# Output-projection units inside an SSM scan's end, and a re-ordered index stage with the first attention pair in it

## The reference

```
first block, layer 0 (mamba2):  z, xbc, dt = split(rmsnorm(x) @ w_in);  xbc = silu(conv4(xbc))
    y  = chunked scan over 4 chunks of 128 tokens, 8 groups of 4 heads, + d_skip * xs
    out = rmsnorm(y * silu(z)) * gate_norm @ w_out          # 2048 -> 1024, "ssm_out"
second block, layer 1 (sparse attention, 528 tokens = 16 meta + 512):
    q, k, v, qi, ki, wi = split(rms_norm(h) @ w_in)         # 16 heads of 64; 8 index heads of 64
    score = sum_h relu(qi_h . ki / 8) * wi_h                # causal; the 16 meta tokens always win
    top   = the 128 best keys of each query;  softmax attention over these alone
```

## Time and profile before

| | us |
|---|---|
| median of three timed runs | 2241.99 (2241.15 to 2243.61) |
| the profiled execution | 2250.37 |
| its span, first to last instruction | 2248.6 |
| TensorE busy | 2140.4 |
| VectorE busy | 1460.2 |
| ScalarE busy | 1022.7 |

### The profile page before, as it was taken

The page is one execution under the profiler, slowest core; times in us unless marked ns, Lnnn a source line. Parts: engine busy times, 40 slices in busy tenths (PEclk is TensorE's granted clock), DMA queues, the critical chain, the costliest instruction groups (busy, mean ns, idle before and its releaser), DMA issues. The chain is left out here.

```text
span 2248.6 us, 40146 instructions
## 1 busy us (share of the span) xinstructions
PE 2140.4 (95%) x14761; PEld 1871.6 (83%) x14761; DVE 1460.2 (65%) x3068; ACT 1022.7 (45%) x1893; POOL 79.3 (4%) x101
## 2 busy tenths in 40 slices
PE   6999999999999799999999999989999999999998
PEld 4777777777767688889999999977877789999886
DVE  6687877537775777776676653369467776666632
ACT  4555554435654456665443332324455554443322
POOL 1000000000000011100000000122100000000000
PEclk9999999999999999999999999988999999999999
DMA  5533331253211222222333243401111213333331
GB/s 129 137 99 104 97 93 52 75 112 66 48 38 57 66 76 66 69 82 58 90 88 93 84 113 88 99 19 38 53 38 37 75 48 95 93 93 90 106 90 50
DMA packets 354767, 174.71 MB, mean 78 GB/s; under 512 B 61055, under 2 KB 350696, under 8 KB 354664
## 3 DMA queue, kind: packets, MB, share of 16 engines
q1 hardware_dynamic: 351976, 168.19, 27.3%
q0 software_dynamic: 2688, 5.20, 1.0%
HBM read 166.58 MB, written 2.16 MB: 75 GB/s over the span
## 5 line engine op out<-in xcount | busy, mean ns | idle before, releaser
L307 PE MATMUL ps<-h_parts,parts 128*128 128x264 f32 (+3 forms) x8576 | 1307.5, 311 | 18.7 <-DVE h_parts L682 6.3
L307 PEld LDWEIGHTS ps<-h_parts,parts 128*128 128x128 f32 x8576 | 1171.3, 190 | 112.0 <-issue 19.4
L266 ACT ACTIVATE parts<-ring 128x1024 fp32r<-128x1024 f32 (+1 forms) x284 | 309.3, 1092 | 648.0 <-PE ps L307 457.0
L282 DVE TENSOR_TENSOR parts<-ring,parts 128x1024 fp32r<-128x1024 f32 (+1 forms) x268 | 339.2, 1268 | 166.0 <-ACT parts L266 165.1
L307 PE MATMUL ps<-wide_parts,parts 128*128 128x512 f32 (+1 forms) x720 | 245.6, 341 | 0.0
L307 PE MATMUL ps<-up_hidden,parts 128*128 128x264 f32 (+1 forms) x1056 | 241.4, 322 | 1.8 <-PEq L2791 1.8
L307 PEld LDWEIGHTS ps<-up_hidden,parts 128*128 128x128 f32 x1056 | 175.1, 188 | 17.4 <-issue 2.1
L2774 DVE TENSOR_TENSOR up_u<-ps,norm_rstd 128x264 f32<-128x264 f32 (+2 forms) x176 | 74.8, 426 | 160.5 <-PE ps L307 153.1
L307 PEld LDWEIGHTS ps<-wide_parts,parts 128*128 128x128 f32 x720 | 136.1, 189 | 16.1
L307 PE MATMUL ps<-gated_high,parts 128*128 128x512 f32 x256 | 82.2, 401 | 3.9 <-DVE wide_parts L1249 3.2
L3104 DVE TENSOR_TENSOR res<-ps,res 128x264 f32<-128x264 f32 (+2 forms) x72 | 31.4, 455 | 83.2 <-PE ps L307 69.3
(11 more groups left out here) (327 smaller groups left out, 2518.9 us busy)
## 6 DMA issues: line engine op xcount, KB each, us to landing
ring<-in_ffn_w_up SPq DMA_DIRECT2D x88, 512.0 KB, 3.8
ring<-in_ssm_w_in SPq DMA_DIRECT2D x48, 512.0 KB, 4.0
ring<-in_ffn_w_down SPq DMA_DIRECT2D x32, 704.0 KB, 4.6
ring<-in_da_w_qkv SPq DMA_DIRECT2D x24, 512.0 KB, 4.0
ring<-in_dsa_w_in SPq DMA_DIRECT2D x24, 512.0 KB, 3.7
ring<-in_att_w_in SPq DMA_DIRECT2D x40, 256.0 KB, 3.7
ssm_prefix<-prefix_rows SPq DMA_DIRECT2D x32, 256.0 KB, 4.1
ring<-in_ssm_w_out SPq DMA_DIRECT2D x16, 512.0 KB, 3.7
```

Of the source, the lines that this page charges most:

```text
L266: self.nc.scalar.activation(self.part(st, u, 0), self.slot(x, st.kt), ACT.Copy).then_inc(self.w_high, 1)
L282: self.nc.vector.tensor_tensor(self.part(st, u, 1), self.slot(u % st.ring, st.kt), self.part(st, u, 0).bitcast(F32), ALU.subtract).then_in ...
L307: m = self.nc.tensor.matmul(out, w[:, n], b, start=start and f == j == 0, stop=stop and f == st.kt - 1 and j == 2)
```

## The change

Three parts. (1) The output projection of the state space layer becomes one stream of 16 units with six ring slots and its own order of units, places and banks (`Gated`). Its first two weight units are split in the last step with projection. In the last scan step, behind each chunk, ScalarE and VectorE make two of the scaled high and low tiles; TensorE multiplies units 0 and 1 two k-tiles at a time before the chunks 2 to 4 in place of warming matmuls, and after the last chunk the rest of them and unit 2. `gated_product` does the other 13 units. (2) In the index stage the value products are spread between the scores in the order of TensorE's stream; the fifth rotation has banks of its own and does not wait for VectorE; GpSimd's value splits from the second on wait for the last rotation; the first pair's projection (`first_pair`) goes ahead of the last value transposition. The order of GpSimd's mask moves and splits changes. (3) For the first query tile, which has 128 keys and the 16 meta keys, the 16 lowest keys are dropped in 2 rounds (weights negated, keys in reverse so that ties fall the same way) where 112 were taken in 14. The core of the diff:

```diff
+class Gated:
+    UNITS = [(0, 0), (1, 0), (2, 0), (3, 0), (0, 1), (1, 1), (2, 1), (3, 1)] + [(t, part) for t in range(4, KT) for part in range(2)]
+    PAIRS = [0, 1, 2, 0, 1, 2, 0, 1, 2, 0, 1, 2, 0, 2, 0, 1]
+    BANKS = [0, 1, 4, 2, 0, 1, 4, 2]
+    def __init__(self, k, st, src, gain, high, low):
+        self.k, self.st, self.src, self.gain = k, st, src, gain
+        self.spread = Spread(k, 2 * KT, None, high, low)
+        self.base, self.half = k.projected, k.halved
+        k.projected += KT
+        k.halved += KT
...
+    def act(self, act, f):
+        k = self.k
+        k.nc.scalar.activation(self.spread.high(f), self.src(f), ACT.Copy, scale=k.col(self.gain + f)).then_inc(k.nsem["high"], 1)
+    def dve(self, dve, f):
+        k, s = self.k, self.spread
+        dve.wait_ge(k.nsem["high"], s.base["high"] + f + 1)
+        k.nc.vector.scalar_tensor_tensor(s.low(f), self.src(f), k.col(self.gain + f), s.high(f).bitcast(F32),
+                                         ALU.mult, ALU.subtract).then_inc(k.nsem["low"], 1)
+    def multiply(self, pe, u, tiles, free):
+        k, (t, part) = self.k, self.UNITS[u]
+        xs = self.spread.parts(0, SEQ)
+        if tiles[0] == 0:
+            k.split_ready(pe, self.st, 0, u)
+            if part == 0:
+                free(u)
+        for f in tiles:
+            self.spread.ready(pe, part * KT + f)
+            m = k.product(self.st, u, k.ps[:, self.BANKS[t], :], lambda g: xs(part * KT + g), start=part == 0, stop=part == 1, tiles=[f])
+        if tiles[-1] == KT - 1:
+            m.then_inc(k.project_done if part else k.project_half, 1)
+    def before(self, u):
+        return max(x for x in range(u) if self.PAIRS[x] == self.PAIRS[u])
+    def high_after(self, act, u):
+        self.wait_unit(act, self.before(u))
+        self.k.high(act, self.st, (0, u))
...
+            norm.pe(pe)
+            for u in range(3, len(units)):
+                begun.multiply(pe, u, range(KT), free)
+            k.keep_warm(3, 16)
...
+            begun.high_after(act, 4)
+            nc.scalar.preload_act_table_set("natural_log_exp_and_others")
+            for f in range(KT, 2 * KT):
+                begun.act(act, f)
+                if f == KT + 1:
+                    norm.rms(act, 0, SEQ, 6, 1)
+            begun.high_after(act, 5)
+            for u in range(4, len(units)):
+                t, part = units[u]
+                if u + 2 < len(units):
+                    begun.high_after(act, u + 2)
...
+            k.low_on_vector(dve, st, (0, 4))
+            for f in range(KT, 2 * KT):
+                begun.dve(dve, f)
+            k.low_on_vector(dve, st, (0, 5))
+            nc.vector.memset(k.acc[:], 0.0).then_inc(n["accumulated"], 1)
+            dve.wait_ge(n["accumulated"], b_acc + 1)
+            dve.wait_ge(n["rstd_steps"], norm.base["rstd_steps"] + 2)
+            for u in range(4, len(units)):
+                t, part = units[u]
+                if u + 2 < len(units):
+                    k.low_on_vector(dve, st, (0, u + 2))
...
+                    if c == 0:
+                        for u in range(3):
+                            sp.wait_ge(k.w_low, st.first + st.units * (st.iterations - 1) + u + 1)
+                            k.load(sp, nxt, 0, u)
                     prefix(GROUPS - 1, c)
                 sp.wait_ge(k.w_low, st.first + st.units * st.iterations)
-                for u in range(nxt.units):
+                for u in range(3, nxt.ring):
...
-                            if 1 <= p <= 4 and not lin:
+                            if p == 1 and not lin:
                                 k.keep_warm(4, 18)
+                            if 2 <= p <= 4 and not lin:
+                                for u in range(2):
+                                    begun.multiply(pe, u, (2 * p - 4, 2 * p - 3), left)
...
-                k.keep_warm(4, 40)
+                for u in range(2):
+                    begun.multiply(pe, u, (6, 7), left)
+                begun.multiply(pe, 2, range(KT), left)
...
+                def next_high(i, u):
+                    at = st.after(i, u, st.depth)
+                    if at is not None:
+                        k.high(act, st, at)
+                    elif u < 5:
+                        k.high(act, nxt, (0, u - 3))
...
+                            if not lin:
+                                begun.act(act, 2 * p - 2), begun.act(act, 2 * p - 1)
+                            if not lin and p == 2:
+                                k.high(act, nxt, (0, 2))
+                            if not lin and p == 4:
+                                begun.high_after(act, 3)
...
                             chunk(i - 1, p - 1)
+                            if not lin:
+                                begun.dve(dve, 2 * p - 2), begun.dve(dve, 2 * p - 1)
                         if lin:
                             conv(i, p - 1)
                             if scan or p >= 3:
-                                k.low_on_vector(dve, st, st.after(i, p - 1, st.depth))
+                                next_low(i, p - 1)
+                    if scan and not lin:
+                        k.low_on_vector(dve, nxt, (0, 2))
...
-                    for m in range(1, 4):
-                        move(pool, m)
-                    for at in ((0, 0), (0, 1), (1, 0)):
-                        k.low(pool, st, at)
+                    move(pool, 1), move(pool, 2)
+                    k.low(pool, st, (0, 0))
+                    move(pool, 3)
+                    k.low(pool, st, (0, 1)), k.low(pool, st, (1, 0))
                     move(pool, 4)
...
-                    step(0, att=False, tail=False)
+                    pe_first(pe, lambda: step(0, att=False, tail=False))
...
+    def rotated(i):
+        return 6 if i == 4 else 2
...
-        k.low_all(pool, vst)
+        k.low(pool, vst, (0, 0))
+        pool.wait_ge(s_rope, 5)
+        for j in range(1, 8):
+            k.low(pool, vst, divmod(j, 4))
...
-            wait(pe, s_rope, i)
+            if i < 4:
+                wait(pe, s_rope, i)
+            else:
+                pe.wait_ge(s_rtok, 2)
...
+        def score(n, x):
             c = META + P * (n - 1)
+            q = NH * (n - 1) + x
+            h = slice(64 * (x % 2), 64 * (x % 2) + 64)
+            wait(pe, s_rel, q - 1)
+            keys = rop[h, 4, META:META + P * n] if n > 1 else rop[h, 4, META + P - 1:META - 1:-1]
+            nc.tensor.matmul(ps[:, 2 + q % 2, 0:P * n], rop[h, x // 2, c:c + P], keys, start=True, stop=True).then_inc(s_s, 1)
+        whole = range(KT)
+        pe.wait_ge(s_r, 1)
+        values(0, 0, whole)
+        pe.wait_ge(s_free, 2 * st.units)
+        for t in range(1, 5):
+            m = nc.tensor.transpose(ps[:, 0, (t - 1) * P:t * P], wiT[:, META + (t - 1) * P:META + t * P], k.ident)
+        m.then_inc(s_wip, 1)
+        pe.wait_ge(s_rope, 5)
+        for x in range(NH):
+            score(1, x)
+            values(0, 1, whole[x:x + 1])
+        for n in range(2, 5):
+            j = 2 * n - 3
+            if n > 2:
+                values(j - 1, 0, whole), values(j - 1, 1, whole)
+                values_transposed(j - 2)
             for x in range(NH):
-                q = NH * (n - 1) + x
-                h = slice(64 * (x % 2), 64 * (x % 2) + 64)
-                wait(pe, s_rel, q - 1)
-                nc.tensor.matmul(ps[:, 2 + q % 2, 0:P * n], rop[h, x // 2, c:c + P], rop[h, 4, META:META + P * n], start=True, stop=True).then_inc(s_s, 1)
-        scores(1)
-        for n in range(1, 5):
-            if n < 4:
-                scores(n + 1)
-            if n == 1:
-                pe.wait_ge(s_acc, 1)
-            for j in values_after[n]:
-                values(j)
-                if j:
-                    values_transposed(j - 1)
+                score(n, x)
+                values(j, x // 4, whole[x % 4 * 2:x % 4 * 2 + 2])
+            values_transposed(j - 1)
+        for j in (6, 7):
+            values(j, 0, whole), values(j, 1, whole)
+            values_transposed(j - 1)
+        first_pair()
...
+        def take_values(j, b):
+            act.wait_ge(s_vdone, 2 * j + b + 1)
+            wait(act, s_vtr, j - 1)
+            nc.scalar.activation(vT[:, j % 2, b * HALF:(b + 1) * HALF], ps[:, 4 + b, 0:HALF], ACT.Copy).then_inc(s_vfree, 1)
+            if b:
+                k.high(act, *((vst, divmod(j + 2, 4)) if j + 2 < 8 else (nxt, (0, j - 6))))
+        take_values(0, 0)
+        for x in range(NH):
+            relu(1, x)
+        take_values(0, 1)
+        for n in range(2, 5):
+            j = 2 * n - 3
+            if n > 2:
+                take_values(j - 1, 0), take_values(j - 1, 1)
+                store_values(j - 2)
             for x in range(NH):
-                q = NH * (n - 1) + x
-                act.wait_ge(s_s, q + 1)
-                wait(act, s_acc, q - NH + 1)
```

(61 more changed lines are left out.)

107 lines of the change are left out of this document (75 added, 32 removed).

## The result

The changed kernel takes 2220.88 us (median of four runs, 2218.84 to 2222.21), the kernel before took 2241.62 beside it: a ratio of 0.9905, 95% interval 0.9888 to 0.9922, 21 us gained. Forecast was 2203.8 with a range of 2192 to 2219: the sign is right, the size is about half of the 38.2 us, and the time lies outside the range. The profiled execution takes 2222.21 us, its span is 2220.4.

The account below looks back on a forecast made before the run. TensorE, busy for 95% of the span, was taken as the bound, with time to win at the scan's end and in the index stage. Gains of 12.2 and 26.0 make 38.2 us: 2241.99 becomes 2203.8 us, range 2192 to 2219.

Parts of the forecast that it names:

- The scan's end: End of the state space layer's scan and output projection: chunks grow by 6.2 us in all, unit 3 starts at 412.1, gain 12.2 us.
- The earlier start of the scores: Index stage: fifth rotation no longer waits and the second value low is kept off, so scores start 1.65 us earlier.
- Dropping 16 keys: Index stage, first query tile: 2 rounds and not 14 save 8.6 us of VectorE; the reversed read costs 0.
- The interleaved scores: Index stage: TensorE's list of values, scores and first pair sums to 80.4 us, next unit 3.0, rotation 26.7 us earlier.
- Who is last: End of the index stage: VectorE is the later chain, done at 1577.2, its first rotation 26.0 us earlier; TensorE's 26.7.
- The blocking by GpSimd: Index stage: GpSimd's lows of units 5 and 7 hold VectorE's score sums, adding 1.9 and 1.7 us; one-input instructions aren't held.
- From the profile to the median: Whole kernel: the full 38.2 us gain was taken from the timed median of 2241.99, 8.4 below the profiled execution.
- (4): Rival, score loops of tiles 1 and 2: clock stays at 1.2 GHz, 26.7 us becomes 13, 2217 us; chance 0.08.
- (6): Rival, index stage: first pair still comes last behind late GpSimd splits, only 8.6+1.65 us stay, 2220 us; chance 0.02.
- (1): Rival, scan's end: lows slip into VectorE's idle 1.47 us and chunks don't grow, gain 18.4 there, 2197.6 us; chance 0.10.
- (2): Rival, scan's end: chain grows by 9 us or over, or unit 3 waits, gain 5 there, 2211 us; chance 0.08.
- (3): Rival, index stage: GpSimd blocks VectorE at each of seven lows, 17 us and not 3.6, 2217 us; chance 0.07.

## Why the prediction was wrong, point by point
**The scan's end: right.** Chunks grew by 5.7 us (forecast 6.2: 2.4, 1.7 and 1.7 where I had 2.5, 1.9 and 1.9, which is 6.3), unit 3 starts at 410.97 (412.1), the part gave 13.0 us (12.2), and TensorE waits for no weights behind it. The reason, highs that come behind the exponentials in ScalarE's order, was shown by moving them: 5.3 us came back.

**The earlier start of the scores: right.** The first score starts at 1480.55. Less the 13.0 us of the scan it would have been at 1482.2, so the fifth rotation and the kept-off low gave 1.6 us (1.65).

**Dropping 16 keys: right in size, and worth nothing alone.** Two rounds, no sign of a cost of the reversed read (the maxima of 128 keys take 0.29 us, as in the earlier trace rows); alone it changes no time. In the changed kernel it counts: VectorE is ready for the rotation at 1571.95 and gets it at 1578.10, so 8.6 us more would have made it last by some 2.5 us (an estimate from these rows; no run has the new order with 14 rounds).

**The interleaved scores: the step that failed.** The price of a score was right (0.21 to 0.85 us). The 32 excursions from products of 128 rows to scores of 64 rows and back cost 0.20 + 0.18 us each, which the sum had at nothing: 12.2 us. The last unit took 4.5 us at a lower clock and not 3.0: 1.5 more. Together 13.7, and the rest of the list was 0.7 us shorter than summed: 96.4 us for 83.4. Scores stretched between the products, which the prediction had named as a sign of being wrong. The bound for the score, up to 1.13 us for 0.85, was applied to the score alone. No row of before shows a lone score between products, but the pair stage shows the excursion itself. TensorE, kernel before:

```profile
1607.79 0.49 PE L2093 MATMUL ps<-wide 64*128 64x128 f32 x4 [0.75 <-DVE wide L2418]
1608.21 1.73 PE L307 MATMUL ps<-h_parts,parts 128*128 128x264 f32 x12
1609.86 0.70 PE L2093 MATMUL ps<-wide 64*128 64x256 f32 x4
```

Two scores of 128 keys on different halves take 0.42 us from start to products, twice the 0.21 of the price, and the 12 products behind them 1.65 us where 12 x 0.125 is 1.50. So some 0.21 and 0.15 us an excursion could have been read before the change was run.

**Who is last: wrong.** VectorE was to be last at 1577.2 in the time of before; it ended at 1570.59 + 13.0 = 1583.6, since tile 1 and 2 are paced by the slower scores. TensorE's chain grew by 13 us and passed it. The blocking by GpSimd was priced at 3.6 us and took 1.3 + 1.7 + 2.1 = 5.0, on other instructions than I named: the first weighting (1.57 us for 0.29) and the mask write of tile 1, which read one SBUF tensor and which I had held for safe, and the mask addition of tile 4 (2.37 for 0.29), which reads two. Behind TensorE's chain it cost nothing.

**From the profile to the median: a second miss.** I took the whole gain from the median. The profiled execution of before stood 8.8 us over its median here, that of after 1.3 over its own: of 28.2 us between the profiles, 7.4 don't appear between the medians. Where they come from is open. The clock behind the wait in the sliding-window stage isn't it, as both profiled executions lose there (18.27 and 18.39 us). The medians of before beside the later runs, on other chips, are 2246.0 and 2244.4 us and not 2241.6, and beside one of them the changed kernel gained 24.4 and not 20.7. The sum of the misses is 26.0 - 13.7 = 12.3 in the index stage, -0.8 in the scan, -1.5 behind them, 7.4 here: 17.4 us, for the 17.1 by which the forecast was off; that it balances follows from how the terms are taken.

**The rivals.** None happened as written. The clock stayed at its full level in the score loops, so (4) is out; the first pair went ahead (6); the chunks grew as forecast, (1) and (2) are out; the blocking of (3) happened in part, off the path. The times of (3) and (4), 2217, and of (6), 2220, are near the result only by number; (6) also counted on 8.6 us from the dropped keys, which bring nothing in the old order.

## What to carry to other kernels
When matmuls of different shape are interleaved, price the change between them, not only the matmuls: count the excursions, and put several small ones behind each other, on different halves of the rows where that is possible. A step whose result another engine waits for belongs ahead of longer work of its own engine that nobody waits for yet. And when a gain makes another engine last, re-price that engine's blocked instructions, since they come out of their cover then.

## What the runs showed of the hardware
- A change of the stationary between 64 rows and 128 rows costs TensorE 0.20 us into the scores and 0.18 us back, each about the time of one fp32 weight load (0.19 us), which starts only with the first matmul of the other shape; two scores on the same 64 rows pay nothing between them.
- Two scores on different halves of the rows take the time of one: 1.06 us for two of 512 keys, against 1.91 on the same half. So it was for 14 of 16 pairs; two took some 0.4 us more.
- GpSimd's subtraction of 128x1024 (2.37 us) holds up a VectorE `tensor_scalar` with one SBUF tensor input: 1.90 us instead of 0.23.
- Behind a wait of over 2 us the granted clock sometimes falls and sometimes doesn't, in two executions of the same kernel behind the same wait of 2.64 us: 72 matmuls took 18.39 us in one and 16.88 in the other.
